# One decoder step with 32 experts: the samples' gather in bf16 parts, the last four experts outside the loop, two units of weights loaded ahead

## What is computed

```python
def moe(xf, w_router, b_router, w1, b1, w2, b2):
    logits = xf.astype(F32) @ w_router.astype(F32) + b_router.astype(F32)
    top_v, top_e = lax.top_k(logits, TOP_K)
    gates = jax.nn.softmax(top_v, axis=-1)
    ...
    def run_block(args):
        e, toks, g = args
        xb = xf[toks]
        h = xb @ w1[e] + b1[e]
        glu = jnp.minimum(h[:, ::2], SWIGLU_LIMIT)
        lin = jnp.clip(h[:, 1::2], -SWIGLU_LIMIT, SWIGLU_LIMIT)
        a = glu * jax.nn.sigmoid(SWIGLU_ALPHA * glu) * (lin + 1)
        out = a @ w2[e] + b2[e]
        return out * g[:, None].astype(out.dtype)
    ...
x1 = layer_norm(DN_ALPHA * x + mix, ln1_g, ln1_b)
x2 = layer_norm(DN_ALPHA * x1 + moe(x1), ln2_g, ln2_b)
y = x2 + jax.nn.sigmoid(x2 @ w_ple_gate) * (p.astype(x2.dtype) @ w_ple)
```

## Time and profile before

| | us |
|---|---|
| median of three runs | 1114.68 |
| lowest and highest | 1113.35, 1115.10 |
| the profiled execution | 1113.78 |
| its span, first to last instruction | 1112.0 |
| TensorE busy | 1096.1 |
| VectorE busy | 409.0 |
| ScalarE busy | 165.3 |
| GpSimd busy | 78.7 |

### The profile page before, as it was taken

How to read it: one execution, slowest core, us unless ns; L and a number is a source line. 1 busy time by engine, 2 the same in 40 slices (tenths; PEclk the granted TensorE clock), 3 DMA queues, 4 the chain that set the end, 5 groups by cost and what they waited for, 6 DMA issues and landing times.

```text
span 1112.0 us, 14748 instructions
## 1 busy us (share of the span) xinstructions
PE 1096.1 (99%) x5674; PEld 423.5 (38%) x5674; DVE 409.0 (37%) x881; ACT 165.3 (15%) x310; POOL 78.7 (7%) x103
## 2 busy tenths in 40 slices
PE   8999999999999999999999999999999999999998
PEld 6886433333333333333333333333333333332344
DVE  1737763333333333333333333333333333323255
ACT  1622330001000100010001000100001000100043
POOL 0847410000000000000000000000000000000000
PEclk9999999999999999999999999999999999999999
DMA  9988889999999999999999999999999999999971
GB/s 315 266 314 336 255 336 421 426 427 427 430 427 430 427 430 427 428 429 427 429 429 428 429 428 428 427 431 427 428 429 428 429 428 428 427 430 428 428 282 39
DMA packets 48723, 440.43 MB, mean 396 GB/s; under 512 B 10513, under 2 KB 13837, under 8 KB 23766
## 3 DMA queue, kind: packets, MB, share of 16 engines
q1 hardware_dynamic: 47657, 437.43, 94.9%
q0 software_dynamic: 896, 2.66, 0.7%
q10 hardware_dynamic: 148, 0.07, 0.0%
HBM read 436.61 MB, written 3.77 MB: 396 GB/s over the span
## 4 chain that ended last, share of the span: by engine, by line
PE 81%; DMA 11%; SPq 5%; DVE 2%; POOL 1%; issue 0%; ACT 0%; DVEq 0%; POOLq 0%
PE bank L904 36%; PE bank L946 18%; DMA ring<-in_w_mlp 9%; PE bank L843 7%; PE bank L865 5%; PE bank L1022 3%; PE bank L708 2%; PE bank L878 2%; PE bank L928 2%; SPq L356 1%; PE bank L891 1%; POOL ring L1912 1%; PE bank L935 1%; PE bank L871 1%; PE bank L538 1%; DMA q_row<-srow 1%
## 5 line engine op out<-in xcount | busy, mean ns | idle before, releaser
L904 PE MATMUL bank<-ring,proj 128*64 128x512 f32 x2048 | 466.0, 597 | 4.5 <-DMA ring<-in_w_mlp 4.5
L1429 DVE SCALAR_TENSOR_TENSOR xT<-bank,proj,xT 128x512 f32<-128x512 f32 x128 | 90.2, 747 | 440.9 <-PE bank L865 439.6
L904 PEld LDWEIGHTS bank<-ring,proj 128*64 128x64 f32 x2048 | 135.5, 136 | 288.2 <-issue 247.4
L946 PE MATMUL bank<-ring,wpool 128*64 128x512 f32 x1024 | 225.1, 592 | 0.0
L946 PEld LDWEIGHTS bank<-ring,wpool 128*64 128x64 f32 x1024 | 71.2, 137 | 129.9 <-issue 129.0
L1777 ACT ACTIVATE proj<-proj 128x256 f32<-128x256 f32 x64 | 26.7, 416 | 546.5 <-DVE proj L1458 546.5
L843 PE MATMUL bank<-xreg,proj 128*64 128x512 f32 (+1 forms) x396 | 95.4, 599 | 0.1
L538 PE MATMUL bank<-xT,ring 128*128 128x264 f32 x320 | 73.9, 388 | 1.7 <-DMA ring<-in_w_in 1.7
L865 PE MATMUL bank<-mixT 64*128 64x512 f32 x264 | 74.5, 641 | 0.5 <-ACT mixT L1785 0.5
L538 PEld LDWEIGHTS bank<-xT,ring 128*128 128x128 f32 x320 | 60.0, 190 | 13.4 <-issue 3.4
L1785 ACT COPY mixT<-bank 128x512 f32<-128x512 f32 x32 | 18.7, 585 | 232.3 <-PE bank L946 232.3
(11 more groups left out here) (334 smaller groups left out, 624.7 us busy)
## 6 DMA issues: line engine op xcount, KB each, us to landing
ring<-in_w_mlp SPq DMA_DIRECT2D x192, 2048.0 KB, 23.5
ring<-in_w_in SPq DMA_DIRECT2D x10, 1024.0 KB, 13.6
ring<-in_w_out SPq DMA_DIRECT2D x4, 1024.0 KB, 8.3
ring<-in_w_ple_gate SPq DMA_DIRECT2D x4, 1024.0 KB, 28.0
xreg<-in_x_prompt SPq DMA_DIRECT2D x4, 512.0 KB, 4.3
ring<-q_row SPq DMA_DIRECT2D x1, 2048.0 KB, 6.9
ring<-k_row SPq DMA_DIRECT2D x1, 2048.0 KB, 6.7
out<-ring POOLq DMA_DIRECT2D x1, 2048.0 KB, 17.6
```

The costliest lines, as they stand in the source:

```text
L904: last = pe.matmul(bank[q][BLOCK * t:BLOCK * (t + 1), :], xgT[:, k % 4, k // 4, :], ring[:, s, col:col + 512], start=False, stop=(k == KD ...
L946: last = pe.matmul(bank[4][BLOCK * h:BLOCK * (h + 1), :], aT[:, m, BLOCK * t:BLOCK * (t + 1)], w[:, k % 2, 512 * h:512 * h + 512], start=F ...
L1429: ins = STT(total[:, c, s], ins_bank[h][:, :], gate_table[:, c, bass.ds(n, 1)], total[:, c, s], ALU.mult, ALU.add)
```

## The change

1. The gather's third chunk, the samples, is done in bf16. Each float32 value is split into three bf16 parts (high, mid, rest) that lie in the partitions 0, 32 and 64 of one tile, and one product with a one-hot of 96 rows adds them. The parts are made once, ahead of the loop, by ScalarE and GpSimd; the very first gather stays in float32.
2. The last four experts are taken out of the loop, on every engine. The last one has no gather, spread or turning of a next expert's rows.
3. Units 0 and 1 of expert 31 are loaded ahead of the loop, into a new tile and into `lnreg`. Units 6, 7 and 10, 11 of expert 31 are loaded as single units. The new tile takes 8 KB a partition; it comes from the rows `urow` and `srow`, which share a tile now, and from the room for GpSimd's DMA descriptors, 8192 to 2048 bytes.
4. So `lnreg` is not free for the scales: ln1's is loaded to `total` by ScalarE's queue after the last part of the router, and `begin_sum` of chunk 0 comes after that of the samples; ln2's rows go to slot 15 of the ring at the end.
5. The sample state is stored by SP instead of GpSimd, right behind the pair of units that waits for the same event. VectorE clears a part of the samples' tile, and the reload of the samples waits for it.

```diff
+SINGLES = (6, 10)
...
+        late = [sb("late", [P, SLOT])[:, :], lnreg[:, 0:SLOT]]
...
+        sample_parts = xtok[0:3 * 32, 2, :].bitcast(BF16)[:, 0:D]
+        part_high = sig.rearrange("p q f -> p (q f)")[0:SAMPLES, :].bitcast(BF16)
+        part_mid = act_out[0:SAMPLES, :].bitcast(BF16)
...
+            def load_late(u):
+                sp.dma_start(late[u], unit_weights(EXPERTS - 1, u)).then_inc(sem("late_in"), 16)
...
+            sp.wait_ge(sem("rest_cleared"), 1)
             sp.dma_start(xtok[0:SAMPLES, 2, :], x_sample[:, 0, :]).then_inc(sem("x_again"), 16)
             sp.wait_ge(sem("tile_ps"), 20)
             load_next(4)
+            load_late(0)
...
             sp.wait_ge(sem("Cnew_done"), 1)
             load_next(10)
-            sp.wait_ge(sem("hT_ps"), 2)
-            sp.dma_start(lnreg[:, 0:D], ln1_g.partition_broadcast(P).rearrange("p o d -> p (o d)"))\
-              .then_inc(sem("ln1_in"), 16)
+            sp.dma_start(C_sample[0].rearrange("b h v k -> v (b h) k"), Cst).then_inc(sem("C_out"), 16)
+            sp.wait_ge(sem("cfin_ps"), 2)
+            load_late(1)
             sp.wait_ge(sem("shT_done"), 1)
             sp.dma_start(early_wple, w_ple[0].rearrange("(k p) n -> p k n", p=P)).then_inc(sem("ple_in"), 16)
             sp.wait_ge(sem("C_out"), 16)
...
                 for n in range(0, UNITS * STEP, 2):
+                    j, u = divmod(n, UNITS)
+                    single = closing and j == STEP - 1 and u in SINGLES
+                    if closing and j == STEP - 1 and u < len(late):
+                        continue
                     sp.wait_ge(sem("units_used"), done + (n - SLOTS + 2))
-                    load_pair(e + n // UNITS, n // UNITS, n % UNITS)
+                    if single:
+                        for a in range(2):
+                            s = slot_of(n + a)
+                            sp.dma_start(ring[:, s, :], unit_weights(e + j, u + a)).then_inc(sem(f"slot{s}"), 16)
+                    else:
+                        load_pair(e + j, j, u)
...
+            load_body(last, used - STEP * UNITS, True)
...
+            wait_slot(15)
             for i, src in enumerate((ln2_g, ln2_b)):
-                sp.dma_start(lnreg[:, D * i:D * i + D], src.partition_broadcast(P).rearrange("p o d -> p (o d)"))\
+                sp.dma_start(ring[:, 15, D * i:D * i + D], src.partition_broadcast(P).rearrange("p o d -> p (o d)"))\
...
                 for c, (_, m) in enumerate(CHUNKS):
                     for h in range(2):
-                        last = pe.matmul(bank[2][BLOCK * h:BLOCK * (h + 1), :], onehot[0:m, c, 0:BLOCK],
-                                         xtok[0:m, c, 512 * h:512 * h + 512], start=(c == 0), stop=(c == 2))
+                        if c < 2 or n is None:
+                            where, rows_ = onehot[0:m, c, 0:BLOCK], xtok[0:m, c, 512 * h:512 * h + 512]
+                        else:
+                            where, rows_ = onehot16, sample_parts[:, 512 * h:512 * h + 512]
+                        last = pe.matmul(bank[2][BLOCK * h:BLOCK * (h + 1), :], where, rows_, start=(c == 0), stop=(c == 2))
...
+                    if final_one and k < len(late):
+                        pe.wait_ge(sem("late_in"), 16 * len(late))
+                        rows_ = late[k]
...
-                pe.wait_ge(sem("onehot_ready"), n * 2 + 4)
-                gather(n + 1)
-                pe.wait_ge(sem("hotT_done"), n + 1)
-                spread_places((j + 1) % 2)
+                if not final_one:
+                    if j == 0:
+                        pe.wait_ge(sem("sample_moved"), 11)
+                    pe.wait_ge(sem("onehot_ready"), n * 3 + 5)
+                    gather(n + 1)
+                    pe.wait_ge(sem("hotT_done"), n + 1)
+                    spread_places((j + 1) % 2)
...
-                pe.wait_ge(sem("xg_copied"), n + 2)
-                turn_gathered()
+                if not final_one:
+                    pe.wait_ge(sem("xg_copied"), n + 2)
+                    turn_gathered()
...
+            for j in range(STEP):
+                expert(npass * EXPERTS - STEP + j, j, True)
...
+            dve.memset(xtok[:, 2, 0:D // 2], 0.0).then_inc(sem("rest_cleared"), 1)
...
+                if chunks == 2:
+                    TT(onehot16, cst[0:3 * 32, C_SLOT:C_SLOT + BLOCK],
+                       pos_table[0:3 * 32, 2, bass.ds(n, 1)].to_broadcast([3 * 32, BLOCK]), ALU.is_equal)\
+                      .then_inc(sem("onehot_ready"), 1)
...
-                one_hot(n + 1, (j + 1) % 2)
+                if j == 0:
+                    dve.wait_ge(sem("sample_moved"), 9)
+                if not final_one:
+                    one_hot(n + 1, (j + 1) % 2)
                 dve.wait_ge(sem("comb_ps"), n * 3 + 3)
-                if j == 0:
-                    dve.wait_ge(sem("sample_moved"), 7)
                 accumulate(2, n, (bank[7], bank[4]))
...
-                step(STT(dst, xtok[0:n, c, :], ALPHA, lnreg[0:n, 0:D], ALU.mult, ALU.mult), name)
-
-            dve.wait_ge(sem("ln1_in"), 16)
-            begin_sum(total[:, 0, :], 0, "total_ready")
+                step(STT(dst, xtok[0:n, c, :], ALPHA, total[0:n, c % 2, :], ALU.mult, ALU.mult), name)
...
             dve.wait_ge(sem("ple_ps"), 3)
+            dve.wait_ge(sem("dve_chain"), counts["dve_chain"])
+            dve.wait_ge(sem("total_in"), 32)
             begin_sum(sample_row, 2, "sample_begun")
+            begin_sum(total[:, 0, :], 0, "total_ready")
             for i in range(3):
                 gates_of(i)
             begin_sum(total[:, 1, :], 1, "total_ready")
...
             parts_out(2)
+            for c in range(2):
+                act.dma_start(total[:, c, :], ln1_g.partition_broadcast(P).rearrange("p o d -> p (o d)"))\
+                   .then_inc(sem("total_in"), 16)
...
                    .then_inc(sem("sample_moved"), 1)
+            act.wait_ge(sem("ple_ps"), 3)
+            act.copy(part_high, xtok[0:SAMPLES, 2, :]).then_inc(sem("part_cast"), 1)
+            for q in range(1, 3):
+                act.copy(pos_table[32 * q:32 * q + SAMPLES, 2, :], pos_table[0:SAMPLES, 2, :])\
+                   .then_inc(sem("sample_moved"), 1)
+            act.wait_ge(sem("part_rest"), 1)
+            act.copy(part_mid, xtok[0:SAMPLES, 2, :]).then_inc(sem("part_cast"), 1)
+            act.wait_ge(sem("part_cast"), 2)
+            act.copy(sample_parts[32:32 + SAMPLES, :], part_mid).then_inc(sem("sample_moved"), 1)
+            act.wait_ge(sem("part_rest"), 2)
+            act.copy(sample_parts[0:SAMPLES, :], part_high).then_inc(sem("sample_moved"), 1)
+            act.wait_ge(sem("sample_moved"), 11)
             act.wait_ge(sem("passes_ready"), 1)
             npass = act.value_load(extra[0:1, 0:1], min_val=0, max_val=PASSES - 1) + 1
...
+            rows_ = xtok[0:SAMPLES, 2, :]
+            pool.wait_ge(sem("sample_begun"), 1)
+            pool.wait_ge(sem("gathered"), 1)
+            pool.wait_ge(sem("part_cast"), 1)
+            pool.tensor_tensor(rows_, rows_, part_high, ALU.subtract).then_inc(sem("part_rest"), 1)
+            pool.wait_ge(sem("part_cast"), 2)
+            pool.tensor_tensor(sample_parts[64:64 + SAMPLES, :], rows_, part_mid, ALU.subtract).then_inc(sem("part_rest"), 1)
```

106 lines of the change are left out of this document (65 added, 41 removed).

## The result

The changed kernel takes 1126.58 us in the median of four runs (1125.16 to 1127.11), the kernel before 1114.89 beside it: a ratio of 1.0104, with a 95% interval of 1.0092 to 1.0116. It is slower by 11.7 us where +4.2 was forecast, and lies above the range, which ended at 1122.9. The profiled execution took 1126.71 us, its span 1124.9, against 1113.78 and 1112.0.

What follows compares the result with a forecast made beforehand. The prediction took the unbroken stream of weight loads as the bound. Stall 4.5, lost latency 0.5 and last expert -0.84 gave +4.2 us, a median of 1118.9 us, range 1113.7 to 1122.9.

Steps and rivals of the forecast that it cites:

- The bound: Whole loop: loads take 29.4 us an expert, TensorE 28.46; a delay in expert 0 moves the end.
- The gather in bf16: Each expert's gather: 0.7 us less TensorE work, but the transposes wait for VectorE, so gain 0.
- The last experts outside the loop: Last expert drops its gather (2.82 us), spread and turning; transposes still wait for VectorE: 0, or at most 0.1.
- Two units early: Expert 31: units 2 to 11 land 4.9 us earlier, removing one TensorE wait at 1051.67; gain 0.84 us.
- The landing T: Ahead of the loop: when ln1's scale has landed, 151.2 to 155.9, taken as 153.5.
- Rival 1: Start of the loop is cheap: T 151.2, S 1 to 2.2, about 1116 us; chance 0.26.
- The line behind T: Start of the loop: sums, copies, casts and subtractions make ScalarE ready for its first sigmoid at T + 19.3.
- S: Stall in expert 0, T - 149.0: 2.2 us at T = 151.2, 4.5 at 153.5, 6.9 at 155.9.
- 0.5: Stream of loads at expert 0: up to 0.5 us more for load latency that was hidden before.
- Rival 3: Start: subtractions meet VectorE and T is 155.9 or later, or w_ple lands late; 1124 us, chance 0.07.
- The chances: Whole kernel: forecast 0.56, rivals 0.26, 0.11 and 0.07; slower by over 0.2% 0.63, same 0.27, faster 0.10.

Runs made afterwards that it cites:

- e3: Changed kernel plus an unread gather of the usual size on TensorE at the end of the last expert: 1124.12 us (1.0093).
- e8: e7 with the gather in 32 bits as before, so no casts, subtractions or parts: 1115.29 us (1.0009).
- e6: e5 with the gather in 32 bits, an unread gather at the last expert's end, and both early units used by expert 28: 1125.05 us (1.0084).
- e10: e8 plus an unread gather at the last expert's end, and its one early unit used by expert 28 instead of 31: 1112.23 us (0.9979).
- e11: e5, but the pair of slots 10 and 11 too is asked for only after ln1's scale: 1118.94 us (1.0043).
- e5: Changed kernel with slots 0 to 3 asked for only after ln1's scale, and C_sample's store issued by ScalarE instead of SP: 1128.72 us (1.0127).
- e12: Changed kernel with the edits of e1 and e2 together: 1129.36 us (1.0124).
- e1: Changed kernel with C_sample's store through GpSimd's queue again, in four pieces, instead of SP's: 1123.26 us (1.0084).
- e2: Changed kernel with the two rows of ln1's shift asked for ahead of ln1's scale on ScalarE's queue: 1126.31 us (1.0106).
- x1: Kernel before the change with only C_sample's store moved from GpSimd to SP: 1115.06 us beside 1115.02 (0.9998).
- e7: Changed kernel with ln1's scale loaded early into lnreg again and only one early unit for expert 31: 1116.91 us (1.0028).

## Why the prediction was wrong, point by point

**The bound: right.** The stream of loads is the limit, and a delay in expert 0 is carried to the end: 10.06 us at expert 0's combine, 10.3 at expert 31's unit 6.

**The gather in bf16: right.** The gather starts at 519.60 in an expert of the middle and the transposes at 522.63, a distance of 3.03 us; it was 512.62 - 509.58 = 3.04.

```profile
519.60 1.89 PE L879 MATMUL bank<-xreg,proj 128*64 128x512 f32 x8
521.31 0.39 PE L879 MATMUL bank<-xreg,onehot 96*64 96x512 bf16 x2
521.63 0.28 PE L892 MATMUL bank<-place_parts,sel 64*128 64x264 bf16 x1
522.63 0.66 PE L979 MATMUL bank<-cst,proj 128*128 128x128 f32 x4 [0.72 <-DVE proj L1525]
```

About 0.8 us of work went (the gather takes 2.03 us to the next matmul instead of 2.82) and 0.72 of idle came; over 31 experts this idle is 23 us in all. "A shorter gather only lengthens that idle time" held to a hundredth.

**The last experts outside the loop: wrong, "0 again, or at most 0.1".** The step priced TensorE's idle time at nothing because the transposes wait for VectorE in any case. They do: from unit 6 of expert 31 to the transposes it is 6.50 us, as it was 6.52. But TensorE now stands idle for 2.85 us of them, and what came behind ran in part at half clock: 2.6 us in the profiled execution. e3 gave back 2.2 us of it. That the idle time is the cause is likely, not certain: the same idle time left the clock full in e8, and the slow layer of e6 came without it.

**Two units early: right in size, wrong in kind.** The wait at 1051.67 is gone. That the price of the second unit is `lnreg`, and with it T, stood in the forecast; that one unit gives the same 0.84 did not, and e10 shows a better place for it.

**The landing T: the step that failed.** The sum put it at 152.8 to 155.9 and took 153.5; it was 159.7. Four things in that step were wrong.
First, it counted bytes up to 152 and shared the stretch among them as if all had been asked for in time. The request itself moved: TensorE stood 2.23 us for `w_ple` at 142.53 and then ran at half clock, so ScalarE asked for the scale at 144.98. In e11, where TensorE didn't wait, it asked at 140.49: 4.5 us.
Second, the forecast let 3.1 us come back because the store is "moved to SP's faster queue". The store did land sooner, after 14.7 us instead of 17.6, and the pair behind it was asked for at 131.76 instead of 133.13. But behind the store the next issue took SP 4.69 us, and `w_ple` went out at 128.41 instead of 123.57.

```profile
117.06 0.44 SPq L460 DMA_DIRECT2D out<-ring  x1
123.67 4.69 SPq L440 DMA_DIRECT2D lnreg<-in_w_mlp  x1
128.41 1.56 SPq L464 DMA_DIRECT2D proj<-in_w_ple  x1
```

A row of the kernel before had the sign of it: the state's load, of the same 4,096 short rows, is on SP's queue at 42.73, and the issue behind it took 6.79 us.

```profile
42.73 1.09 SPq L384 DMA_DIRECT2D ring<-in_state_mlstm_C  x1
43.86 6.79 SPq L385 DMA_DIRECT2D wrout<-in_w_router  x1
```

Third, the stretch from 133.5 to 137.5 had little to give back. Its row has 88 GB/s, but also a DMA share of 0.95: the engines' time was taken though few bytes moved. Now it moved 246 GB/s, and the stretch from 137.5 to 152 moved 390 where it was 407.
Fourth, and largest: the landing isn't bytes over rate. From its first request the scale took 14.7 us here and 9.2 in e11, 5.5 us for what else was in flight.

Why it is so slow beside pairs is only argued. Its packets are smaller. The DMA view of 144 to 160 us, ScalarE's queue (packets, MB, share of 16 engines), and that of 300 to 400 us, weights alone:

```profile
q10 hardware_dynamic: 292, 1.05, 16.1%
```

```profile
q1 hardware_dynamic: 2944, 42.86, 100.7%
```

That is 3.6 KB a packet against 14.6 (both means, with small packets among them). Rival 1 drew the opposite from the Trainium skill, "DMA: Bandwidth & Descriptors", "Queues, rings and completion order": that each engine takes its queues in turn, packet by packet, was read as if the scale would come early. By that rule a queue with packets of a fourth of the size gets a fifth of the bytes, if the profile's packets are those of the page; this is an estimate, and at 428 GB/s it gives 12.2 us for the scale's 1.05 MB. The 14.7 us of the changed kernel are near it, the 16.8 of e5 and 21.3 of e12 are longer. No run changed the size of a packet, so this share isn't shown. Serving requests in their order wouldn't do: one pair ahead of the scale and the scale itself are 3.1 MB, by estimate 7.4 us at this rate, and e5 took 16.8. Nor is it shown why a lead of 1.2 us (e1) is enough.

**The line behind T: right.** 19.17 us instead of 19.3; the casts took 1.04 (1.05 forecast), the subtractions 2.13 (2.3). The slow 8x160 product came again, 1.76 us beside 0.69 for a 128x160 one, and again VectorE began a sum of 128x1024 (163.56) while it ran. So no run tells the port pair that the prediction cites from a product that is slow by itself; the subtractions, for which the range left room for 1 us more, were not slow. The formula S = T - 149.0 gives 10.8 for the true T, and 10.5 was measured (the transposes at 181.74, in place of 171.21); with 0.5, -0.84 and the 2.6 of expert 31 the sum is 1113.8 + 13.1 = 1126.9, beside 1126.71 measured.

That this comes out so well is in part luck. TensorE was 10.06 us late by a way that the formula doesn't have: its wait for `w_ple`, its wait for the rows of ln1's shift behind the scale, and half clock behind both. With this way shortened (e2) the formula's line alone gives 10.9 us; with the line taken out (e6) the other way alone gives 13.4, and in e5 it gives 11.5 where the formula has 8.1. The two ways happened to end together here. Both hang on the scale's request: the one waits for the scale, the other for the rows behind it.

**The chances.** Rival 3 named T at 155.9 or later with a late `w_ple`, gave 1124 us and 0.07. Its T was the case, its slow subtractions were not. The upper bound of 155.9 came from bytes alone and held no delay of the request; the prediction gives no other reason for so small a chance.

## What to carry to other kernels

Before you price the landing of a small load as bytes over rate, look at what is in flight in the other queues and at who waits for what stands behind it: here the place of one request was worth 9 us. Before an idle stretch of TensorE is priced at nothing, add what the clock may do behind it. And where the loads are the bound, memory for one unit ahead was worth more here in front of the first of the late waits than of the last (2.2 us, e10).

## What the runs showed of the hardware

Not expected: after 2.85 us of idle TensorE's second layer of 32 instructions took 9.27 us instead of 7.09, part of it at the lower of the two clocks (1.2 instead of 2.4 GHz); 8.78, 8.22 and 7.89 in other kernels, and 7.09 in e8 after the same idle time. In e6, without that idle time, it took 8.78, and the granted clock of 1072 to 1076 us was 0.63. At the start the granted clock was 0.50 in 144 to 148 us after 2.23 us of idle at 142.53. Here are 4 us each, with the columns of the earlier trace rows:

```profile
140.00:144.00 4.00, 1.77 (x23) 0.84 (x25) 2.64 (x8) 0.78 (x2) 0.00 (x0) 0.87 1.08 452
144.00:148.00 4.00, 4.00 (x33) 2.41 (x26) 1.54 (x7) 2.04 (x4) 0.00 (x0) 0.50 0.98 414
...
160.00:164.00 4.00, 4.00 (x12) 1.16 (x10) 3.73 (x12) 0.00 (x0) 1.12 (x2) 0.57 0.00 0
```

In x1 1.11 us of idle at the same place changed nothing. The Trainium skill, "TensorE: Matmul & The Clock Gate", section "Part 1: The HAM clock gate", says that the clock is halved by how busy the engine has lately been, and that the moment isn't tied to the program, so that one kernel measures differently from run to run. The spread between e7 and e8, which are alike at this place, and among the ten executions of e11 (0.992 to 1.000) agrees.

Behind a store of 4,096 rows of 512 bytes SP's next issue took long in all nine profiles that have it there, 4.53 (e3) to 5.53 us (x1); in the six where the store is on another queue it took 0.33. On ScalarE, whose next request came 24 us later, nothing of it was seen in an issue, but the store took 22.8 to 23.9 us to land, and 14.5 to 18.1 on SP.
